# Two transformer blocks on one core: a memory-attention head's output is issued ahead of the next head's softmax

## The reference

```
def memory_cross_attention(h, m, w_q, w_kv, q_g, k_g, w_o):
    B, S, _ = h.shape
    q = rmsnorm(heads(h @ w_q, MEM_HEADS), q_g)
    k, v = jnp.split(m @ w_kv, 2, axis=-1)
    k = rmsnorm(heads(k, MEM_HEADS), k_g)
    v = heads(v, MEM_HEADS)
    s = jnp.einsum("bqhd,bkhd->bhqk", q, k).astype(jnp.float32) * MEM_DIM ** -0.5
    p = jax.nn.softmax(s, axis=-1).astype(v.dtype)
    o = jnp.einsum("bhqk,bkhd->bqhd", p, v).reshape(B, S, MEM_W)
    return o @ w_o
```

## Time and profile before

| | us |
|---|---|
| median of 3 runs | 1175.96 (1172.93 to 1177.26) |
| the profiled execution | 1173.07 |
| its span in the trace | 1171.4 |
| PE busy | 1145.2 (98%) |
| DVE busy | 812.5 (69%) |
| ACT busy | 622.3 (53%) |
| POOL busy | 82.1 (7%) |

### The profile page before, as it was taken

The page is one execution under the profiler, slowest core; times in us unless marked ns, Lnnn a source line. Parts: engine busy times, 40 slices in busy tenths (PEclk is TensorE's granted clock), DMA queues, the critical chain, the costliest instruction groups (busy, mean ns, idle before and its releaser), DMA issues.

```text
span 1171.4 us, 16802 instructions
## 1 busy us (share of the span) xinstructions
PE 1145.2 (98%) x6765; PEld 999.7 (85%) x6765; DVE 812.5 (69%) x881; ACT 622.3 (53%) x801; POOL 82.1 (7%) x114
## 2 busy tenths in 40 slices
PE   8999999999999999999999999999999998999997
PEld 7978898889987799999888888888777887888886
DVE  6897658756878568787548777547776747777743
ACT  7666446436478466565345444436456547444432
POOL 7101100200000000000000000002700000000000
PEclk9999999999999999999999999999999999999999
DMA  8654333334665354655655655555633534665560
GB/s 259 190 158 147 99 106 110 109 108 156 220 198 181 108 163 156 204 169 191 216 179 181 210 179 186 200 195 177 201 116 127 180 108 127 194 202 182 179 214 36
DMA packets 144420, 193.95 MB, mean 166 GB/s; under 512 B 6168, under 2 KB 121240, under 8 KB 144344
## 3 DMA queue, kind: packets, MB, share of 16 engines
q1 hardware_dynamic: 143144, 188.43, 49.7%
q0 software_dynamic: 1200, 4.46, 1.1%
HBM read 191.82 MB, written 1.05 MB: 165 GB/s over the span
## 4 chain that ended last, share of the span: by engine, by line
PE 83%; DVE 10%; ACT 4%; issue 2%; DMA 0%; DVEq 0%; ACTq 0%
PE banks L1328 23%; PE banks L1362 19%; PE banks L1310 13%; PE banks L1331 11%; DVE wlo L1920 4%; PE banks L1347 3%; PE banks L1338 2%; PE banks L1589 1%; PE banks L1477 1%; ACT whi L1649 1%; PE banks L1464 1%; PE banks L1376 1%; PE banks L1547 1%; DMA x_tok<-in_x 0%; DVE x_tok L2193 0%
## 5 line engine op out<-in xcount | busy, mean ns | idle before, releaser
L1920 DVE TENSOR_TENSOR wlo<-raw,whi 128x2048 fp32r<-128x2048 f32 (+1 forms) x178 | 406.5, 2291 | 122.5 <-ACT whi L1649 122.4
L1649 ACT ACTIVATE whi<-raw 128x2048 fp32r<-128x2048 f32 (+1 forms) x179 | 340.1, 1903 | 248.3 <-PE banks L1331 146.0
L1328 PE MATMUL banks<-xhl,whi 128*128 128x512 f32 x1232 | 396.2, 403 | 2.7 <-DVE y5l L2248 1.8
L1331 PEld LDWEIGHTS banks<-xhl,wlo 128*128 128x128 f32 x1232 | 231.4, 188 | 54.6
L1331 PE MATMUL banks<-xhl,wlo 128*128 128x256 f32 x1232 | 242.6, 278 | 0.0
L1328 PEld LDWEIGHTS banks<-xhl,whi 128*128 128x128 f32 x1232 | 188.9, 189 | 10.3 <-issue 5.6
L1310 PE MATMUL banks<-xhl,whi 128*128 128x256 f32 x912 | 165.5, 284 | 1.3 <-DVE xhl L1947 0.7
L1310 PEld LDWEIGHTS banks<-xhl,whi 128*128 128x128 f32 x912 | 142.0, 192 | 2.1 <-DVE xhl L1947 1.1
L1310 PE MATMUL banks<-xhl,wlo 128*128 128x256 f32 x456 | 129.0, 283 | 0.0
L1362 PE MATMUL banks<-whi,hh 128*128 128x512 f32 x264 | 102.9, 390 | 0.0
L1362 PE MATMUL banks<-wlo,hh 128*128 128x512 f32 x264 | 102.7, 389 | 0.0
(11 more groups left out here) (368 smaller groups left out, 1531.9 us busy)
## 6 DMA issues: line engine op xcount, KB each, us to landing
raw<-in_w_in SPq DMA_DIRECT2D x40, 1024.0 KB, 5.3
raw<-in_w_up SPq DMA_DIRECT2D x22, 1024.0 KB, 5.8
raw<-in_ffn_w_gate SPq DMA_DIRECT2D x22, 1024.0 KB, 5.3
raw<-in_ffn_w_up SPq DMA_DIRECT2D x22, 1024.0 KB, 5.3
raw<-in_ffn_w_down SPq DMA_DIRECT2D x22, 1024.0 KB, 5.0
raw<-in_w_down SPq DMA_DIRECT2D x11, 1024.0 KB, 5.6
raw<-in_w_out SPq DMA_DIRECT2D x8, 1024.0 KB, 5.2
raw<-in_xa_wkv SPq DMA_DIRECT2D x8, 1024.0 KB, 5.7
```

Source lines behind the costliest of these rows:

```text
L1328: pe.matmul(bank(b[m]), wh[:, k, m * P:(m + 1) * P], both[:, k, :, :].rearrange("p a t -> p (a t)"), start=(k == 0), stop=(k == KD - 1), s ...
L1331: ins = pe.matmul(bank(b[m])[:, 0:T], wl[:, k, m * P:(m + 1) * P], Xh[:, k, :], start=False, stop=(k == KD - 1), skip_group_check=True)
L1649: act.activation(columns(whi, c, part), columns(raw, c, part), ACT.Copy).then_inc(act_done, 1)
L1920: dve.tensor_tensor(columns(wlo, c, part), columns(raw, c, part), columns(whi, c, part), ALU.subtract).then_inc(dve_done, 1)
```

## The change

For the kind `mem` alone, the links of a lane are cut otherwise. Before, the link that holds `pt(h)` also held `sc`, `sm` and `ex` of the lane's next head, and the link of the output `pv`, `oc`, `ol` of head h held the next head's `pn` in its middle. Now `pt(h)` keeps only `sc` of the next head beside it, the output link of head h comes first and `sm`, `ex` of the next head follow in it, and `pn` of the next head is a link of its own. Also, where a chunk needs steps that are in no order yet, `hook` now takes only those chains that hold one of these steps (`until`), plus those that fit, instead of all.

```diff
-    def hook(force=False):
-
-        chosen = [chain for chain in side if chain and (force or fits(chain))]
+    def hook(force=False, until=()):
+
+        chosen = [chain for chain in side if chain and (force or fits(chain) or any(s[1:] in until for link_ in chain for s in link_ if not callable(s)))]
...
         while any(step not in pl.number for step in pl.ready[c]) and side:
-            hook(True)
+            hook(until=[step for step in pl.ready[c] if step not in pl.number])
...
-            if nxt is not None:
+            if nxt is not None and kind in ("mem",):
+                turn_.insert(1, ("pe", "sc", kind, nxt))
+                out_ += [("dve", "sm", kind, nxt), ("act", "ex", kind, nxt)]
+            elif nxt is not None:
                 turn_ = [turn_[0], ("pe", "sc", kind, nxt), turn_[1], ("dve", "sm", kind, nxt), ("act", "ex", kind, nxt)]
                 out_.insert(1, ("dve", "pn", kind, nxt))
             links += [turn_, out_]
+            if nxt is not None and kind in ("mem",):
+                links += [[("dve", "pn", kind, nxt)]]
         return links
```

## The result

| | before | changed |
|---|---|---|
| median | 1174.59 us (20 runs) | 1177.86 us (20 runs) |
| lowest to highest | 1172.93 to 1177.26 | 1177.21 to 1180.42 |
| profiled execution | 1173.07 | 1177.30 |
| its span | 1171.4 | 1175.6 |

The ratio is 1.0032, with a 95% interval of 1.0025 to 1.0039. The change makes the kernel 0.32% slower, some 3.8 us (the medians alone differ by 3.3): less than the 0.5% that I had set as the bound for a difference, but clear of noise with this many runs. Of the 20 runs of the change 11 lie within 1177.2 to 1178.2, the others near 1179.5 and 1180.4; those of before lie near 1173.0, 1174.5 and 1176.0, and one at 1177.3. The forecast was +0.38% and 1180.4 us, the range 1176.5 to 1183.5.

The account below looks back on a forecast made before the run. PE, busy in 98% of the span, was taken to bound the kernel. 0.41 - 1.34 + 1.53 + 3.82 = +4.42 us on the median of 1175.96 gave 1180.4 us (0.38% more), range 1176.5 to 1183.5.

Parts of the forecast that it names:

- Term 1: Start of chunk 51 on PE: 0.41 us later, as ol(1) stands behind ex(2), hi(52), lo(52) and add(50).
- Term 2: Chunk 51 on PE: holds one pv instead of pt(3), pv(2) and pv(3), 6.45 us instead of 7.79, -1.34.
- Term 3: pt(3) on PE after chunk 51: waits 1.53 us for pn(3), which stands behind lo(53) on DVE.
- the sign that I had named: PE at pt(3): the forecast would be wrong if pt(3) does not wait; a wait of about 1.5 us was forecast.
- Term 4: End of head 3, pt(3) to chunk 52: nothing left to put beside the chain, 3.82 us.
- the pn(3) rival: At pt(3): pn(3) is in time and the wait for it vanishes, +2.9 us, 1178.9 us; chance 0.14.
- The clock rival: Thin stretch from 405.24 to 410.59: the clock falls and costs 1.6 us more, +6.0, 1182.0 us; chance 0.32.
- My own reading: Clock in PE's thin stretches: what is thin as a whole counts for a fall, not one gap.
- the faster case: Chunks 51 and 52: the 2.22 us stall goes whole and chunk 52 does not wait, -2.2 us, 1173.7; chance 0.04.

Follow-up runs that it names:

- experiment 12: The changed kernel, unchanged, profiled a second time: 1182.25 us.
- experiment 7: Changed kernel with extra matmuls, results not used, in PE's waits before chunk 51, pv(3) and chunk 52: ratio 1.0029, median 1176.96 us.
- experiment 5: Kernel before with head 1's output put ahead: oc(1) before ex(3) and pc(2) on ACT, ol(1) before pn(3) on DVE: ratio 0.9993, median 1173.31 us.
- Experiment 6: Kernel before, reordered so that critical steps lead on DVE, ACT and PE: ratio 0.9980, median 1172.09 us.
- experiment 2: Changed kernel with pt(3) and pv(3) back between quarters of chunk 51 and pn(3) right behind sm(3): ratio 1.0003, median 1174.73 us.
- experiment 3: Changed kernel with pn(3) alone moved, right behind sm(3) on DVE: ratio 1.0027, median 1176.95 us.
- experiment 4: Changed kernel with pt(3) and pv(3) back between quarters of chunk 51, pn(3) left behind the remainder of chunk 53: ratio 1.0038, median 1178.71 us.
- experiment 8: Kernel before with only the new rule for forcing steps, the links of the memory attention as before: ratio 1.0010, median 1175.99 us.
- experiment 1: Kernel before with only pt(3) and pv(3) moved on PE, behind the last quarter of chunk 51: ratio 1.0028, median 1177.91 us.
- experiment 9: Kernel before with 11 extra matmuls, results not used, in PE's wait before chunk 51: ratio 0.9994, median 1172.99 us.

## Why the prediction was right

**Term 1, the start of chunk 51, +0.41.** It is +0.21 in the rows (398.59 against 398.38); with both counted from pt(0), which came 0.08 earlier, +0.29 (383.22 in the change, 383.30 before). The mechanism is as put: ol(1) no longer waits behind sm(3) and pn(3), but behind a chain through ex(2), hi(52), lo(52) and add(50), with the two waits of DVE forecast at those places. The steps and handovers have the forecast lengths (sm(2) at 390.48 to chunk 51 at 398.59 is 8.11 for 8.09). What is off is the start: I took DVE as free of sm(1) at 385.81, but that row is the start of sm(2), and lo(51) now follows sm(1) at 385.60.

**Term 2, chunk 51 shorter by its pieces, -1.34.** In experiment 12, with the clock up, PE comes to the end of chunk 51 at about 405.02 (the last start, 404.79, and 0.23): 6.47 us, for a forecast of 6.45.

**Term 3, the wait for pn(3), +1.53.** 1.16 there (405.02 to 406.18), of which the row counts 1.01 as idle. Most of the difference is a handover counted twice: pt(3) starts 0.87 behind pn(3) (405.31 to 406.18), where I had 0.86 for the step and 0.26 more. In the first profile the slow quarter of chunk 51 took the place of the wait, so the sign that I had named, that pt(3) does not wait, came up there although the chain behind it was as forecast (pn(3) at 405.71).

**Term 4, the bare end of head 3, 3.82.** 3.68 (406.58 to 410.26): pt(3) to pv(3) 1.40 for 1.54, pv(3) to chunk 52 2.28 for 2.28. The handover that no row had shown was 0.14 shorter than taken. The idle that the rows count is less than I forecast: 5.4 us in experiment 12 (2.48, 1.01, 0.74 and 1.15) for 6.9, since the rows of pt(3) and pv(3), 0.66 and 1.13 us long in the first profile, last longer than the 1.1 us in all that I had set for them. The starts do not depend on that.

**The sum.** 0.29 - 1.32 + 1.16 + 3.68 = 3.8 us with the clock up, where I had 4.4. The terms come from two profiles (1 and 4 from the first, 2 and 3 from experiment 12), and their sum is what experiment 7 shows (chunk 52 at 409.83 with pt(0) at 383.16, so 3.8 later than before) and the size of the measured ratio. With the fall at 398 it is 4.2, as in the profile of the change.

**The absolute time.** 1180.4 was 2.5 us over the measured median, which by itself lies nearer to the 1178.9 of the pn(3) rival; it is the rows, not this figure, that bear the forecast out. The median of three runs that I started from was 1.4 over the median of 20; the terms were 0.6 too large in sum; I put the rest, 0.5, down to how often the clock falls in either kernel, which is not shown. The size of the ratio came out near the forecast partly by luck: in the first profile 0.4 us of clock made up for most of the 0.6 that the terms were too large.

**The clock rival.** The mechanism exists and its price was set too low: the clock can fall in the thin stretch, and then costs 2.6 us (2.14 in chunk 52, 0.47 behind pv(3)), not 1.6, since it stayed at half for about twice as long as in the earlier trace rows. By the rule of the Trainium skill (TensorE: Matmul & The Clock Gate, section "Why this matters for your kernels"), long unbroken gaps are what to avoid; here the clock fell in one profile behind a single wait of 2.48 us, and in the other not behind the same wait but in a stretch of waits of 1.01, 0.74 and 1.15 us. None of these is as long as the gaps it warns of, so keeping to that rule did not keep the clock up here. My own reading, that what is thin as a whole counts and not one gap, does not cover the fall behind the single wait of 2.48 us either. What I missed is the wait before chunk 51 as the place, which the change makes longer (2.48 us for 2.22), and that a fall in front of another wait is mostly paid for already.

**The pn(3) and the faster case** did not come. The bound for the latter held with pv(1) in its place: experiment 5 gained 0.96 us where I had 0.97 as the most that pv(1) allows. Experiment 6 gained more, 2.4 us at chunk 52, by work put into the wait and by moving pv(1).

## What to carry to other kernels

In an in-order schedule, ask of each step not only what it may lead but what is left to run beside the handovers behind it. The last head of such a chain needs other work between its steps on the engine that bounds the kernel; with all of that work put ahead of it, the 3.7 us from pt(3) to chunk 52 lay bare, and PE did nothing else in them. To let an output lead, move it ahead of the two or three steps that stand in its way, and check which large transfers or conversions slide behind a wait as a result.

## What the runs showed of the hardware

The same program, with the same wait of 2.48 us on PE, had its granted clock halved behind that wait in one execution and not in another, where it fell ten microseconds later for twice as long. Over all profiles, the clock fell behind the wait before chunk 51 in five of the six in which that wait took 2.48 or 2.66 us (the change and experiments 2, 3, 4 and 8; not 12), and in none of the four in which it took 2.2 us (the kernel before three times, and experiment 1). With the wait shortened to 1.26 or 0.18 us or filled with matmuls (experiments 5, 6, 7 and 9) it did not fall there either. The length of the wait does not decide alone: in the three profiles of the kernel before, the clock fell behind a wait of 1.6 us near 977 and not behind the one of 2.2 us near 398.

Runs of one kernel lie in steps of about 1.5 us, and the slower ones have the lower mean clock: of the runs of the kernel before, those with a mean of 0.998 took 1172.7 to 1173.3 us, those with 0.993 or 0.994 took 1176.2 to 1177.1. One fall costs about as much as a step where nothing takes it up (1.4 us in chunk 51 of the changed kernel), so I take the steps for a count of falls; which fall makes which step was not shown. A kernel with more thin stretches, as in experiment 1, had its profiled execution 2.3 us and its median 3.6 us over the kernel before. A profile of a run of one step should not be held against one of another without counting the falls.
